# Sparse attention takes its token tiles from the last to the first, and the merge takes the last group of tokens first

## What is computed

```python
def dsa_attention(q, k, v, ...):           # 8 query heads, 2 key heads, head size 64
    sc = where(chosen, q @ k.T * scale, -inf)
    return softmax(sc) @ v

h = rms_norm(x); proj = h @ w_in           # q, k, v, gates and index inputs
oa = mla_attention(...) * silu(gate_a)
ob = dsa_attention(...) * silu(gate_b)
x1 = x + (sigmoid(m_a) * (oa @ w_branch_mla) + sigmoid(m_b) * (ob @ w_branch_dsa)) @ w_out
x2 = second_block(x1)
```

## Time and profile before

| | |
|---|---|
| time of the runs | 3273.33 us median of 3 (3270.79 to 3274.34) |
| time of the profiled execution | 3276.11 us |
| its span in the profile | 3274.3 us |
| PE busy | 3105.3 us (95%) |
| DVE, ACT, POOL busy | 2043.0, 1834.2, 821.9 us |
| mean granted TensorE clock | 0.979 of full speed |
| index stage's last matmul ends, merge's first begins | at 1555.06 us and 2003.86 us of the span |

### The profile page before, as it was taken

How to read it: one execution, slowest core, us unless ns; L and a number is a source line. 1 busy time by engine, 2 the same in 40 slices (tenths; PEclk the granted TensorE clock), 3 DMA queues, 4 the chain that set the end, 5 groups by cost and what they waited for, 6 DMA issues and landing times. The chain is left out here.

```text
span 3274.3 us, 51655 instructions
## 1 busy us (share of the span) xinstructions
PE 3105.3 (95%) x17304; PEld 2646.9 (81%) x17304; DVE 2043.0 (62%) x4805; ACT 1834.2 (56%) x3869; POOL 821.9 (25%) x1234
## 2 busy tenths in 40 slices
PE   6999969999999999999799998999999999989998
PEld 5888858888878877777588777999878888879997
DVE  5767667887855666555689897443456776751112
ACT  5656557777766666664578785211256666642211
POOL 6453511122112121233322112100133334320010
PEclk9999979999999999999899999999999999999999
DMA  4666673535342222233531103444442222243332
GB/s 172 207 194 208 186 179 71 121 73 126 102 183 78 75 81 77 76 94 90 135 87 45 32 20 124 158 155 138 152 142 57 76 74 58 87 161 117 111 126 78
DMA packets 307575, 370.48 MB, mean 113 GB/s; under 512 B 24832, under 2 KB 252080, under 8 KB 303344
## 3 DMA queue, kind: packets, MB, share of 16 engines
q1 hardware_dynamic: 292272, 319.72, 33.6%
q0 software_dynamic: 13152, 46.32, 4.4%
q10 hardware_dynamic: 1888, 1.15, 0.1%
HBM read 216.32 MB, written 150.80 MB: 112 GB/s over the span
## 5 line engine op out<-in xcount | busy, mean ns | idle before, releaser
L93 PE MATMUL i_p_g<-i_hT_lo,i_wh 128*128 128x512 f32 x768 | 307.8, 401 | 6.3 <-PEq L70 6.3
L95 PE MATMUL i_p_g<-i_hT_hi,i_wh 128*128 128x512 f32 x768 | 305.6, 398 | 0.0
L94 PE MATMUL i_p_g<-i_hT_hi,i_wl 128*128 128x512 f32 x768 | 305.5, 398 | 0.0
L1786 DVE SCALAR_TENSOR_TENSOR i_score<-i_relu,i_w,i_score 128x1024 f32<-128x1024 f32 (+7 forms) x154 | 154.9, 1024 | 168.7 <-ACT i_relu L1666 166.7
L1676 ACT ACTIVATE i_above<-i_score,i_less 128x2048 bf16<-128x2048 f32 (+13 forms) x140 | 183.2, 1308 | 106.3 <-POOL i_less L1740 69.9
L1126 DVE TENSOR_TENSOR mla_tl<-mla_p_x,mla_th 128x512 fp32r<-128x512 f32 (+1 forms) x320 | 194.1, 609 | 68.0 <-ACT mla_th L1171 62.1
L1126 DVE TENSOR_TENSOR dsa_tl<-dsa_p_x,dsa_th 128x512 fp32r<-128x512 f32 x272 | 186.7, 689 | 47.6 <-ACT dsa_th L1171 42.2
L1171 ACT ACTIVATE mla_th<-mla_p_x 128x512 fp32r<-128x512 f32 (+1 forms) x320 | 168.0, 528 | 85.3 <-PE mla_p_x L1078 83.0
L1163 ACT ACTIVATE dsa_probs<-dsa_probs,dsa_shift 128x640 f32<-128x640 f32 (+7 forms) x192 | 172.1, 896 | 49.1 <-POOL dsa_shift L1195 46.3
L2237 POOL TENSOR_TENSOR win_probs<-win_probs,win_inv 128x1024 f32<-128x1024 f32 (+1 forms) x64 | 118.8, 1857 | 316.7 <-DVE win_inv L2533 316.7
L1163 ACT ACTIVATE mla_probs<-mla_probs,mla_shift 128x640 f32<-128x640 f32 (+4 forms) x192 | 171.8, 895 | 32.2 <-POOL mla_shift L1195 27.5
(11 more groups left out here) (356 smaller groups left out, 9868.9 us busy)
## 6 DMA issues: line engine op xcount, KB each, us to landing
scratch_gates<-i_ob SPq DMA_DIRECT2D x95, 256.0 KB, 2.4
m_m<-scratch_gates SPq DMA_DIRECT2D x64, 256.0 KB, 4.0
f_hs<-scratch_h2T SPq DMA_DIRECT2D x16, 1024.0 KB, 9.4
scratch_qkT<-b_th SPq DMA_DIRECT2D x64, 192.0 KB, 2.6
i_ws<-in_w_in SPq DMA_DIRECT2D x24, 512.0 KB, 4.6
scratch_qkT<-b_tl SPq DMA_DIRECT2D x60, 192.0 KB, 2.9
b_xt<-in_x SPq DMA_DIRECT2D x16, 512.0 KB, 4.9
scratch_h<-b_xh POOLq DMA_DIRECT2D x16, 512.0 KB, 3.0
```

The costliest lines, as they stand in the source:

```text
L93: pe.matmul(out, l[0], r[1], start=start, stop=False)
L94: pe.matmul(out, l[1], r[0], start=False, stop=False)
L95: return pe.matmul(out, l[0], r[0], start=False, stop=stop)
L1786: nc.vector.scalar_tensor_tensor(out=acc, in0=r, scalar=w[:, t, h:h + 1], in1=acc, op0=ALU.mult, op1=ALU.add).then_inc(summed, 1)
```

## The change

The units of dsa are made from tile 15 down to tile 0, so that unit 0 has 2048 keys and unit 31 has 128. The first unit needs all keys, so both pieces of k low are loaded ahead of the values, and unit 0 waits for both pieces. The first mask rows loaded are those of tiles 15 and 14. The merge takes its groups in the order 7, 0, 1, ..., 6, so that its first group is again one whose outputs come first. `pool_last` moves from the last unit's first block to that of unit 24 (tile 3, key head 0).

```diff
-                elif step[0] == "B" and step[2] == 0 and halved(step[1]):
+                elif step[0] == "B" and step[2] == 0:
                     n = step[1]
-                    n_totaled += 1
-                    pool.wait_ge(exped, n_exp[n, 3])
-                    nc.gpsimd.tensor_tensor(sums[:, n % R, 0], sums[:, n % R, 0], sums[:, n % R, 1],
-                                            ALU.add).then_inc(totaled, 1)
-                    if n == len(units) - 1:
+                    if halved(n):
+                        n_totaled += 1
+                        pool.wait_ge(exped, n_exp[n, 3])
+                        nc.gpsimd.tensor_tensor(sums[:, n % R, 0], sums[:, n % R, 0], sums[:, n % R, 1],
+                                                ALU.add).then_inc(totaled, 1)
+                    if n == len(units) - 8:
                         layer.pool_last(pool)
...
-                    sp.wait_ge(stored, 32)
+                    sp.wait_ge(stored, 64)
                     after.load_early(sp)
...
+    order = tuple(range(NT - 1, -1, -1))
...
-                      for t in range(NT) for g in range(KV)]
+                      for t in self.order for g in range(KV)]
...
+        for x in range(2):
+            self.load_keys(sp, x, self.k_lo, 1)
         for x, at in enumerate(self.pieces):
-            self.load_keys(sp, x, self.k_lo, 1)
             sp.dma_start(self.v[:, at.start // P:at.stop // P].bitcast(F32),
...
-        if n in (0, 4 * KV):
-            pe.wait_ge(self.k_in[n // (4 * KV)], 16 * 4)
+        if n == 0:
+            for k_in in self.k_in:
+                pe.wait_ge(k_in, 16 * 4)
...
+def merge_group(x):
+
+    return (x - 1) % (NT // 2)
...
-                    sp.wait_ge(given.ob_stored[p], 16 * (NT * KV // 2 - (2 if g < n_groups - 1 else 0)))
+                    sp.wait_ge(given.ob_stored[p], 16 * (NT * KV // 2))
...
-            pool.wait_ge(inverted, 2)
+            pool.wait_ge(inverted, 4)
```

More of the change, by code:

```diff
@@ L1899, in load, with load_queries @@
     def load(self, sp, n):
-        t, g = n // KV, n % KV
-        if t < 2 or g:
+        x, g = n // KV, n % KV
+        if x < 2 or g:
             return
-        if t == 2:
+        if x == 2:
             self.index_in.wait_mask(sp)
-        sp.wait_ge(self.sems["moved"], self.sems["n_s"][KV * (t - 1)])
-        self.load_queries(sp, t)
-    def load_queries(self, sp, t):
+        sp.wait_ge(self.sems["moved"], self.sems["n_s"][KV * (x - 1)])
+        self.load_queries(sp, x)
+    def load_queries(self, sp, x):
+        t = self.order[x]
         at, keys = slice(t * P, (t + 1) * P), P * (t + 1)
         for half in range(2):
-            sp.dma_start(self.q[half * HD:(half + 1) * HD, t % 2].bitcast(F32),
+            sp.dma_start(self.q[half * HD:(half + 1) * HD, x % 2].bitcast(F32),
                          self.qbT[half].rearrange("j (r d) t -> d (j r) t", d=HD)[:, :, at])\
-                .then_inc(self.q_in[t % 2], 16)
-        sp.dma_start(self.m[:, t % 2, 0:keys], self.mask[at, 0:keys]).then_inc(self.m_in[t % 2], 16)
+                .then_inc(self.q_in[x % 2], 16)
+        sp.dma_start(self.m[:, x % 2, 0:keys], self.mask[at, 0:keys]).then_inc(self.m_in[x % 2], 16)
     def wait_scores(self, pe, n):
-        t = n // KV
-        pe.wait_ge(self.q_in[t % 2], 32 * (t // 2 + 1))
-        if n in (0, 4 * KV):
-            pe.wait_ge(self.k_in[n // (4 * KV)], 16 * 4)
+        x = n // KV
+        pe.wait_ge(self.q_in[x % 2], 32 * (x // 2 + 1))
+        if n == 0:
+            for k_in in self.k_in:
+                pe.wait_ge(k_in, 16 * 4)
     def wait_values(self, pe, n):
-        if n in (0, 4 * KV):
-            pe.wait_ge(self.v_in[n // (4 * KV)], 16)
+        if n == 0:
+            for v_in in self.v_in:
+                pe.wait_ge(v_in, 16)
     def sync_unit(self, sp, n):
@@ L1972, in store @@
     def store(self, n):
-        t, g = n // KV, n % KV
+        t, g = self.order[n // KV], n % KV
         rows = self.oT[g * 4 * HD:(g + 1) * 4 * HD, t * P:(t + 1) * P]
@@ L2603, in load_x @@
     def load_x(self, sp, t):
-        sp.wait_ge(self.x1_stored[t % 2], 16 * (t // 2 + 1))
+        sp.wait_ge(self.x1_stored[t % 2], 16 * ((t // 2 + 1) % (NT // 2) + 1))
         sp.dma_start(self.xt[:, t % 2], self.x1[t * P:(t + 1) * P, :]).then_inc(self.x_in[t % 2], 16)
@@ L2637, in __init__, with load_o @@
         self.w_in = [nc.alloc_semaphore(name=f"m_w_in{x}") for x in range(2 * KD)]
-    def load_o(self, sp, g, y):
+    def load_o(self, sp, x, y):
+        g = merge_group(x)
         at = slice(g * 2 * P, (g + 1) * 2 * P)
@@ L2723, in stage_merge @@
         block = c.enter_context(nc.Block())
-        rows = lambda t: slice(t * P, (t + 1) * P)
-        tok = lambda g: slice(g * GO, (g + 1) * GO)
+        tile = lambda t: 2 * merge_group(t // 2) + t % 2
+        rows = lambda r: slice(r * P, (r + 1) * P)
+        tok = lambda x: slice(merge_group(x) * GO, (merge_group(x) + 1) * GO)
         early = len(given.early)
@@ L2764, in load_x @@
                     sp.wait_ge(squared, t - 1)
-                sp.dma_start(x[:, t % 2], residual[rows(t), :]).then_inc(x_in[t % 2], 16)
+                sp.dma_start(x[:, t % 2], residual[rows(tile(t)), :]).then_inc(x_in[t % 2], 16)
             def store(t):
                 sp.wait_ge(added, t + 1)
-                sp.dma_start(out[rows(t), :], x[:, t % 2]).then_inc(stored[t % 2], 16)
+                sp.dma_start(out[rows(tile(t)), :], x[:, t % 2]).then_inc(stored[t % 2], 16)
             def load_band(n):
@@ L2961, in invert @@
                 dve.wait_ge(rooted, t + 1)
-                nc.vector.reciprocal(rs[:, t:t + 1], sd[:, t:t + 1]).then_inc(inverted, 1)
+                nc.vector.reciprocal(rs[:, tile(t):tile(t) + 1], sd[:, t:t + 1]).then_inc(inverted, 1)
             def split_band(ch):
```

## The result

The changed kernel takes **3280.91 us** (median of 8 runs, 3278.15 to 3284.52) and the kernel before 3273.5 us (8 runs, 3268.96 to 3276.47): ratio 1.0025, 95% interval [1.0014, 1.0036], so 4.6 to 11.8 us slower. The forecast was 3278 us, slower by 4.3.

What follows compares the result with a forecast made beforehand. The prediction took PE as the bound almost everywhere, counting time lost to idling or lower clock. Start -3.5, middle -4.6 and end +12.4 gave +4.3 us on 3273.3, so 3278 us; range 3265 to 3290.

Steps and rivals of the forecast that it cites:

- Start, -3.5: Start of dsa: later keys and pipeline filling lose 24.8 us instead of 28.3, query waits go; bounds -8 to 0.
- Middle, -4.6: Large units: fewer waits for a PSUM bank, PE losing 9 us instead of 13.6; bounds 0 and -8.
- End, +12.4: Unit 24's first block to the merge: small units with nothing to hide them lose 19 us, not 6.6; bounds +0.4, +17.
- imperfect interleaving: Part of the end's loss: ACT slower than PE in tiles 1 and 0, 3 us for six units up to V29.
- The gating, 1: Gating on POOL ahead of a shift at the end: 4.74 us, about 3.7 covered, price 1 us.
- signs of being right: Expected first-score and first-block times, no long query waits, gating about 45 us before merge, four outputs back to back.
- sign of being wrong: Wrong if key wait is far off 19.6 us, DVE or ACT paces large units, merge waits, or PE's clock falls late.
- Rival 3: End is worse: lower PE clock, uncovered gating or late tile 0 queries add 9 us, 3287 us; chance 0.20.
- Rival 2: The end hides: DVE alone sets the end, which loses under 8 us; -7.7 in all, 3266 us; chance 0.14.
- Rival 4: Terms are small: keys at 1571, bank waits stay, end loses 14 us; about 3271 us; chance 0.16.
- The rule on the shared side of SBUF: End: POOL's last outputs and DVE's splitting exclude each other, costing some 1.6 us more than free overlap; already included.

Runs made afterwards that it cites:

- run 3: Changed kernel with the second tile's queries and mask loaded behind k low instead of ahead of it: 3275.49 us, ratio 1.0006 to the kernel before.
- run 7: run 3 with POOL's output operations for units 22 to 29 taken two shifts later: 3275.62 us, ratio 1.0003 to the kernel before.
- run 10: run 5 plus outputs and multiplications one block behind for units 26 to 31, and POOL's outputs of units 22 to 29 two shifts later: 3264.96 us, ratio 0.9975.
- run 11: run 3 plus early outputs for units 26 to 31, POOL's outputs of units 22 to 29 two shifts later, gating at unit 16: 3271.66 us, ratio 0.9994.
- run 6: run 3 with multiplications and outputs one block behind rather than three for units 26 to 31: 3272.38 us, ratio 0.9991 to the kernel before.
- run 2: Changed kernel with the merge's gating on POOL at unit 16 instead of unit 24: 3283.32 us, ratio 1.0027 to the kernel before.
- run 4: Changed kernel with up to two exps, not one, after a block or V in units of at most 4 blocks: 3294.9 us, ratio 1.0058.
- run 5: run 1 with only v's first piece ahead of tile 15's queries, no wait there for stored mask rows, gating at unit 16: 3271.69 us, ratio 0.9991.
- run 8: run 3 with tiles ordered 15 to 4, then 0 to 3, and outputs and multiplications one block behind from unit 23 on: 3275.66 us, ratio 1.0001.
- run 1: Changed kernel with tiles ordered 0, 1, then 15 to 2, and the merge starting with group 0: 3280.07 us, ratio 1.0021 to the kernel before.

## Why the prediction was right, and where its sum was off

The direction and the main mechanism held: the keys later, the query waits gone, and an end where small units stand alone. The sum was +4.3 and the profiled stage gave +9.9; the end alone was 6.9 us more than its term. That the time came out so near is in part luck: in the two profiled executions the index stage's better clock hid 2.3 us, and the profiled stages can each be 2 to 3 us off by the clock.

- **Start, -3.5; measured -3.8** (18.66 + 15.02 less 9.2 of work, against 28.3). PE waited 18.66 us (19.6 expected) and began its blocks 15.02 us later (14.4). That bytes ahead of k low set the wait is shown by run 3: the second tile's mask and queries, 1.02 MB, moved behind gave 4.9 us back.
- **Middle, -4.6.** PE idled 10.0 us of 370.12 where the prediction had 9 and before's middle 13.6: -3.6. The reason held for half of it. The prediction read 6.5 us of waits for a bank into the earlier trace rows; with those in front of scores they were 6.5 + 1.7, and they are 5.4 + 1.1 now, 1.7 less. The rest is waits for exps (3.6, now 6.1 less the 3.4 of the first block) and for maxima (1.4, now 0.7). Against it stands a term that the prediction does not have: the work after the first block's wait ran at half clock, which run 3 prices at 2.4 us (22.5 and 20.1 us to the first V).
- **End, +12.4; by the prediction's count +19.3.** This is the term that was mis-sized. The prediction counted 48 us from unit 24's first block to the merge, of which 29 were work, and it took 54.9. Up to V29 32.1 rather than 29.2; from V29 to unit 29's output on POOL 12.1 rather than 10; from there to the merge 10.7 rather than 9. Part of the error is the work, not the loss: PE idled 20.1 us, and its 5.71 us of work at a clock of 0.53 lost another 2.7 (an estimate from that row), so 22.8 were lost (+16.2), and the work was 3 us longer than 29.
- **What the end's excess was.** The first piece was called "imperfect interleaving" on ACT, 3 us. Runs 7, 10 and 11 show that POOL's outputs ahead of shifts cost some 4 us up to V29. The other pieces are the outputs and multiplications held back by three blocks, which in units of one block means three units (run 6 gained 3.3 us on run 3; unit 31's spread waiting 3.8 us for unit 29's output belongs to it), and PE's lower clock from 1993.87 on.
- **The gating, 1; measured 0** (run 2). Its cover was enough here and is gone once something else stands beside it on POOL (run 7).
- **The signs.** Of the signs of being right, the first score (18.66 us), the first block (15.0 us), the query waits and PE's 20.1 us of idling at the end came; the gating was 53.8 us ahead of the merge, not 45, and three outputs stood back to back, not four. One sign of being wrong came too: a lower clock in the last 20 us.
- **The rivals.** Rival 3 was to be decided by the end losing over 24 us; by the prediction's count 25.9 were lost, by the rows 22.8. It had the size almost right by partly wrong parts: the clock did fall, but the gating was covered and tile 0's queries were never late. Rival 2 fell: DVE idled too (busy 33.78 of 54.89 us). Rival 4's 3271 does not follow from its own terms: the keys 3.7 us sooner, nothing in the middle and 14 lost at the end make +0.2, so about 3273.5.
- **The rule on the shared side of SBUF.** POOL's two operations took 1.40 and 2.12 us beside DVE's split of `m_o`, and 2.23 for the one that met DVE's `m_bl`, where 0.61 and 1.28 are usual. The Trainium skill (SBUF — State Buffer, "SBUF: two separate sides") has the two engines shut each other out for a whole instruction; the trace agrees in kind. Its cost was in the estimate.
- **The total.** Before's profiled index stage ran 634.8 us from its first matmul to its last, the changed kernel's 631.2, and the other runs' 631.6 to 633.5. Of the 3.6 us, 2.3 are the clock in the last 56 us, which run 4 has at 0.94 with the changed kernel's loads, so chance; another 0.8 is the wait ahead of them (3.71 and 2.94 us). The rest stays open. This is why the span grew less than the stage.

## What to carry to other kernels

Small units of work cost least where the critical engine would idle anyway: here at the start, under the loads (run 5), while with units of 2 to 4 blocks behind them they lost what they lose at the very end (run 8). Turned to the end of a stage they show every fixed distance in the schedule: "three blocks behind" is a few microseconds in a large unit and three whole units in a small one, so such distances belong in the units' own measure. In a strict list a long operation that is not urgent (here 1.9 us of output on POOL) goes behind the short one that feeds the critical engine; an engine busy 53% (29.36 of 54.89 us) can set the pace by its order alone. And the start of a stage under its loads is the right place for units that need little data, if the order of the loads is made for it: run 1 has those units there too, with tile 15's queries behind all of v, and is 0.3% slower than run 5; 7.4 of the 11.2 us of stage lie where the loads set the time.

## What the runs showed of the hardware

- The same wait of 3.40 us ahead of the first block was followed by work at half clock in seven of eight profiles (four transposes in 1.09 to 1.12 us) and at full clock in one (0.66, run 3). The half clock also lasted differently long: over the first 5 us of blocks the mean granted clock was 0.50 in four of them, 0.66 to 0.68 in three and 1.00 in run 3, and the time up to the first V was 22.5 to 22.7, 21.6 to 21.7 and 20.1 us.
- At the end of the index stage the clock scattered too: a wait of 2.74 us was followed by half clock in run 4, and one of 2.94 us by full clock in the changed kernel. The 225 matmuls behind it took 52.88 us at a mean granted clock of 1.00 and 55.24 at 0.94. Between two single profiles of this kernel 2 to 3 us are no evidence.
- Waits much shorter than at the start were followed by the lower clock: 1.07, 1.20 and 1.84 us of idling with little work between them at the changed kernel's end, 1.44 and 1.25 us in run 1. The Trainium skill (TensorE: Matmul & The Clock Gate, Part 1) has the clock set by how busy PE has been recently; these rows agree.
